# A routed expert layer in float32: 64-row units, and 129 to 192 rows of one expert in one body

## The reference

```python
logits = (hf @ router_w) + router_b
top_v, top_i = lax.top_k(logits, 4)             # 32 experts, 4 per token
gates = jax.nn.softmax(top_v, axis=-1)
...
gu = xb @ w_gu[e] + b_gu[e]                     # 1024 -> 2048
gate = jnp.minimum(gu[:, :1024], 7.0)
up = jnp.clip(gu[:, 1024:], -7.0, 7.0)
act = (up + 1.0) * (gate * jax.nn.sigmoid(1.702 * gate))
y = act @ w_down[e] + b_down[e]                 # 1024 -> 1024
out = jnp.zeros((n_tok, d)).at[buf_tok].add(y * buf_w[:, None])
```

## Time and profile before

| | |
|---|---|
| median of 3 runs | 2874.4 us (2848.94 to 2881.16) |
| the profiled execution | 2873.04 us |
| its span, first to last instruction | 2871.3 us |
| PE busy, share of the span | 2514.8 us, 88% |
| PE weight loads busy | 2049.8 us, 71% |
| DVE, ACT, POOL busy | 54%, 41%, 14% |
| mean granted TensorE clock | 0.898 of 2.4 GHz |
| DMA, mean over the span | 201 GB/s |
| stage 6, first matmul to last split | 1054 to 2791 us |

### The profile page before, as it was taken

The page is one execution under the profiler, slowest core; times in us unless marked ns, Lnnn a source line. Parts: engine busy times, 40 slices in busy tenths (PEclk is TensorE's granted clock), DMA queues, the critical chain, the costliest instruction groups (busy, mean ns, idle before and its releaser), DMA issues. The chain is left out here.

```text
span 2871.3 us, 35294 instructions
## 1 busy us (share of the span) xinstructions
PE 2514.8 (88%) x11411; PEld 2049.8 (71%) x11412; DVE 1557.2 (54%) x1705; ACT 1163.9 (41%) x1355; POOL 406.4 (14%) x423
## 2 busy tenths in 40 slices
PE   4899765899959529999999999999999999999980
PEld 4788654677748428888788888888877788878860
DVE  4411075433331425577855585575688755867545
ACT  4112142222221024456644474454566645655430
POOL 1420023110010150001100010000011100101004
PEclk8999888555579759999999999999999999999995
DMA  3132212700023166688976697686799966988658
GB/s 127 68 108 84 85 33 57 282 1 1 0 83 110 63 213 195 212 265 296 364 240 201 206 336 241 202 295 202 259 367 368 359 205 226 360 283 296 227 172 351
DMA packets 429684, 577.36 MB, mean 201 GB/s; under 512 B 28989, under 2 KB 308670, under 8 KB 429630
## 3 DMA queue, kind: packets, MB, share of 16 engines
q1 hardware_dynamic: 414494, 525.25, 55.0%
q0 software_dynamic: 15136, 51.40, 4.7%
HBM read 509.31 MB, written 67.29 MB: 201 GB/s over the span
## 5 line engine op out<-in xcount | busy, mean ns | idle before, releaser
L1386 DVE TENSOR_TENSOR VL<-RAW,VH 128x2048 fp32r<-128x2048 f32 x389 | 883.3, 2286 | 273.6 <-ACT VH L1381 272.7
L1381 ACT ACTIVATE VH<-RAW 128x2048 fp32r<-128x2048 f32 x390 | 728.7, 1912 | 148.2 <-DMA RAW<-in_expert_w_gate_up 92.6
L164 PE MATMUL banks<-VH,TL 128*128 128x512 f32 x1504 | 587.9, 391 | 0.0
L162 PE MATMUL banks<-VH,TH 128*128 128x512 f32 x1504 | 587.4, 391 | 0.0
L163 PE MATMUL banks<-VL,TH 128*128 128x512 f32 x1504 | 586.9, 390 | 0.0
L163 PEld LDWEIGHTS banks<-VL,TH 128*128 128x128 f32 x1504 | 282.8, 188 | 62.0
L164 PEld LDWEIGHTS banks<-VH,TL 128*128 128x128 f32 x1504 | 282.7, 188 | 60.7
L162 PEld LDWEIGHTS banks<-VH,TH 128*128 128x128 f32 x1504 | 283.5, 189 | 54.0
L162 PE MATMUL banks<-VH,AH 128*128 128x512 f32 x752 | 297.4, 395 | 11.7 <-DVE AL L1554 11.7
L164 PE MATMUL banks<-VH,AL 128*128 128x512 f32 x752 | 293.9, 391 | 0.0
L163 PE MATMUL banks<-VL,AH 128*128 128x512 f32 x752 | 293.3, 390 | 0.0
(11 more groups left out here) (276 smaller groups left out, 2874.9 us busy)
## 6 DMA issues: line engine op xcount, KB each, us to landing
RAW<-in_expert_w_gate_up SPq DMA_DIRECT2D x264, 1024.0 KB
RAW<-in_expert_w_down SPq DMA_DIRECT2D x130, 1024.0 KB
dY<-zeros SPq DMA_DIRECT2D x32, 512.0 KB, 10.9
dY<-yb SPq DMA_DIRECT2D x62, 256.0 KB
RAW<-in_w_in SPq DMA_DIRECT2D x6, 2048.0 KB, 8.7
dY<-yb SPq DMA_DIRECT2D x68, 128.0 KB
xin<-in_x SPq DMA_DIRECT2D x8, 512.0 KB
RAW<-in_w_out SPq DMA_DIRECT2D x2, 2048.0 KB
```

Of the source, the lines that this page charges most:

```text
L162: pe.matmul(o, lh, rh, start=start, stop=False)
L164: return pe.matmul(o, ll, rh, start=False, stop=stop)
L1381: act.activation(VH[:, i, ks], RAW[:, i, ks], ACT.Copy).then_inc(s_hi, 1)
L1386: dve.tensor_tensor(VL[:, i, ks], RAW[:, i, ks], VH[:, i, ks].bitcast(f32), ALU.subtract).then_inc(s_w, 1)
```

## The change

Rows are counted in units of 64 instead of blocks of 128. A table entry covers up to three units; an expert with more gets a second entry. An entry with one or two units runs narrow(), which is the one-block body as before. An entry with three units (129 to 192 rows) runs wide(), which takes the place of the two-block body. In wide() the gate and up columns are computed the other way round: 128 weight columns are stationary, and the tokens stream, rounded and rest beside each other (T2 holds both, 2 x 192), so that VH meets 384 columns and VL the 192 rounded ones. The two halves of the sum stand side by side in PSUM. ACT adds the bias to the right one (Identity with a bias per partition, from btT), DVE adds the left one to it (zz). The result has the experts' inner index on the partitions already, so that the transposes L1617 and the gate and up bias matmuls are gone. The down columns are as before, with 128 and then 64 stationary rows (A2). The next entry's tokens are turned in columns 4 and 5 of both bodies, the first 128 and then 64 rows.

The core of the diff:

```diff
+UN = 64
+NW = 3 * UN
+SBMAX = S * TOPK // UN + NE
+SLOTS = (SBMAX + 2) * UN
+SSB = S * TOPK // NW + NE
...
-                for j in range(1, S // P):
-                    link(dve.scalar_tensor_tensor(out=nb[:], in0=cnt, scalar=float(j * P), in1=nb[:], op0=ALU.is_gt, op1=ALU.add))
+                for j in range(1, S // UN):
+                    link(dve.scalar_tensor_tensor(out=nb[:], in0=cnt, scalar=float(j * UN), in1=nb[:], op0=ALU.is_gt, op1=ALU.add))
...
-                for j in range(2, S // P, 2):
+                for j in range(3, S // UN, 3):
...
-                sp.dma_start(tokr[0:SBMAX], dTok.rearrange("(s p) a -> s (p a)", p=P)).then_inc(s_tk, 16)
+                units = dTok.rearrange("(s p) a -> s (p a)", p=UN)
+                for i in range(2):
+                    sp.dma_start(tokr[0:SBMAX, i * UN:(i + 1) * UN], units[i:i + SBMAX]).then_inc(s_tk, 16)
...
+                    pool.tensor_copy(bcur[:], btT[:, :, :, bass.ds(e, 1)].rearrange("p g i a -> p g (i a)")).then_inc(s_bcur, 1)
...
             @block.scalar
+                def pair_hi(s, i):
+                    act.wait_ge(s_a, s * G2 + (2 + i + 1))
+                    act.activation(A2[:, 0, i], qa[:, i % 2, 0:NW], ACT.Copy, scale=1.0 / ALPHA).then_inc(s_ahi, 1)
...
+                def wide(s):
+                    begin(s)
+                    act.wait_ge(s_bcur, s + 1)
+                    for i in range(G2):
+                        b = i % 2
+                        act.wait_ge(s_mm, s * N2 + (i + 1))
+                        act.activation(lo2[:, b, 0], ps[2 * b][:, NW:2 * NW], ACT.Identity, bias=bcur[:, 0, i:i + 1])
+                        act.activation(lo2[:, b, 1], ps[2 * b + 1][:, NW:2 * NW], ACT.Identity, bias=bcur[:, 1, i:i + 1]).then_inc(s_ea, 1)
+                        if i >= 1:
+                            pair_hi(s, i - 1)
+                        act.wait_ge(s_up, s * G2 + (i + 1))
+                        act.activation(sg[:, b, 0:NW], zz[:, b, 0], ACT.Silu, scale=ALPHA).then_inc(s_sg, 1)
+                        if i == G2 - 1:
+                            pair_hi(s, i)
+                        if b == 1:
+                            round_next(s, i // 2)
+                    for c in range(GU, NCH):
+                        tokens_hi(c - GU, s * 2 + (c - GU + 3))
...
             @block.vector
+                def wide(s):
+                    for i in range(G2):
+                        b = i % 2
+                        dve.wait_ge(s_ea, s * N2 + (i + 5))
+                        dve.tensor_tensor(zz[:, b], bank_pairs[b].rearrange("p (g n) -> p g n", g=2)[:, :, 0:NW], lo2[:, b], ALU.add).then_inc(s_up, 1)
+                        dve.wait_ge(s_up, s * G2 + (i + 1))
+                        dve.tensor_scalar(u1[:, b, 0:NW], zz[:, b, 1], LIMIT + 1.0, 1.0 - LIMIT, ALU.min, ALU.max).then_inc(s_clip, 1)
+                        if i >= 1:
+                            pair_lo(s, i - 1)
+                        dve.wait_ge(s_clip, s * G2 + (i + 1))
+                        dve.wait_ge(s_sg, s * G2 + (i + 1))
+                        dve.scalar_tensor_tensor(out=qa[:, b, 0:NW], in0=sg[:, b, 0:NW], scalar=TOP, in1=u1[:, b, 0:NW], op0=ALU.min, op1=ALU.mult).then_inc(s_a, 1)
+                        if i == G2 - 1:
+                            pair_lo(s, i)
+                        if b == 0:
+                            second_half(s, i // 2)
+                        else:
+                            first_half(s, i // 2)
...
             @block.tensor
+                def begin(s):
+                    pe.wait_ge(s_x, s * 2 + 2)
+                    pe.wait_ge(s_hot, s + 1)
...
+                def narrow(s):
+                    begin(s)
+                    for c in range(NCH):
+                        if c >= GU:
+                            tokens(c - GU, s * 16 + 32, s * 2 + (c - GU + 2))
...
+                def wide(s):
+                    begin(s)
+                    for i in range(G2):
+                        c, j = i // 2, i % 2
+                        if i < 2:
+                            pe.wait_ge(s_ea, s * N2 + (2 * i + 2))
+                        else:
+                            pe.wait_ge(s_up, s * G2 + (i - 1))
+                        for k in range(KT):
+                            if j == 0 and k % HK == 0:
+                                pe.wait_ge(s_w, s * N2 + (2 * c + 1 + k // HK))
+                            for g in range(2):
+                                o = ps[2 * j + g]
+                                col = slice(g * HC + j * P, g * HC + (j + 1) * P)
+                                if k == KT - 1:
+                                    pe.matmul(o[:, 0:NW], VL[:, c % 3, k, col], T2[:, 0, k], start=False, stop=False)
+                                last = pe.matmul(o[:, 0:2 * NW].rearrange("p (a n) -> p a n", a=2), VH[:, c % 3, k, col], T2[:, :, k], start=k == 0, stop=k == KT - 1)
+                                if k < KT - 1:
+                                    pe.matmul(o[:, 0:NW], VL[:, c % 3, k, col], T2[:, 0, k], start=False, stop=False)
+                        last.then_inc(s_mm, 1)
+                    pe.sem_inc(s_aT, G2)
```

More of the change, by code:

```diff
@@ L1322, in _ @@
                 pe.matmul(ps[3][:, 0:SSB + 1], ones[:], diag[:], start=True, stop=True).then_inc(s_exp, 1)
-                pe.wait_ge(s_tk, 16)
+                pe.wait_ge(s_bt, 2)
+                for g in range(2):
+                    for i in range(2 * GU):
+                        c, j = i // 2, i % 2
+                        rows, at = slice(64 * (c // 3), 64 * (c // 3) + NE), (c % 3) * CH + g * HC + j * P
+                        q, n = c // 3, 6 - 4 * (c // 3)
+                        last = pe.transpose(ps[4 + q][:, (g * n + i % 6) * NE:(g * n + i % 6 + 1) * NE], braw[rows, at:at + P], ident[rows, rows])
+                last.then_inc(s_bT, 1)
+                pe.wait_ge(s_tk, 32)
                 pe.transpose(ps[2][:, 0:SBMAX], tokr[0:SBMAX], ident[0:SBMAX, 0:SBMAX]).then_inc(s_tT, 1)
@@ L1401, in stage6, with height, superblocks @@
         G2, N2 = 2 * GU, 2 * NCH
-        def items(c, nh):
-            return [(h, c * nh + h) for h in range(nh)]
-        def superblocks(eng, body):
+        def height(h):
+            return P if h == 0 else UN
+        def superblocks(eng, narrow, wide):
             n = eng.value_load(nblk[0:1, 0:1], min_val=1, max_val=SSB)
@@ L1412, in superblocks @@
                     with eng.If(two > 0):
-                        body(s, 2)
+                        wide(s)
                     with eng.Else():
-                        body(s, 1)
+                        narrow(s)
                 with eng.Else():
@@ L1451, in _ @@
                     load(sp, c + 3, e0)
-                n = superblocks(sp, body)
+                n = superblocks(sp, narrow, wide)
                 for i in range(3):
@@ L1542, in _ @@
+                tokens_hi(0, 1)
+                tokens_hi(1, 2)
                 act.activation(warm[:], onec[:], ACT.Silu).then_inc(s_warm, 1)
-                superblocks(act, body)
+                superblocks(act, narrow, wide)
             @block.vector
@@ L1591, in _ @@
                 tokens_lo(0, 1)
-                superblocks(dve, body)
+                tokens_lo(1, 2)
+                superblocks(dve, narrow, wide)
             @block.tensor
@@ L1620, in body, with bias_in, turned @@
[L1620 to L1626 removed]
+                def bias_in(o, c, m):
+                    return pe.matmul(o, hot_e[:, c // 3, 0:m], btab[:, (c % 3) * CH:(c % 3 + 1) * CH], start=True, stop=False)
+                def turned(s, c):
+                    pe.wait_ge(s_a, s * G2 + (2 + (c + 1) * 2))
+                    pe.wait_ge(s_act, s * G2 + (2 + max(0, c - 1) * 2))
+                    for j in range(2):
+                        last = pe.transpose(ps[4 + c % 2][:, j * P:(j + 1) * P], qa[:, c % 2, j * P:(j + 1) * P], ident[:])
+                    last.then_inc(s_aT, 2)
@@ L1659, in _ @@
                 tokens(0, 16)
-                superblocks(pe, body)
+                tokens(1, 16, 1)
+                superblocks(pe, narrow, wide)
     YR = 4
```

318 lines of the change are left out of this document (171 added, 147 removed).

## The result

The changed kernel takes 2750.0 us (median of 4 runs, 2739.7 to 2754.2); the kernel before, with its runs beside it, 2873.8 us (2848.9 to 2881.2). The ratio is 0.957, 95% interval 0.953 to 0.962: 4.3% faster. The forecast was 2736 us in a range of 2695 to 2785.

The account below looks back on a forecast made before the run. PE was taken to bound the two-block bodies, the weights' transfer by DMA the late one-block ones. From 2873.0 us, -169 (wide), +27.5 (narrow) and +4.3 (rest) gave 2736 us, range 2695 to 2785.

Parts of the forecast that it names:

- The wide body: Stage 6, PE-bound: 61.0 us against 72.3 for the two-block body, 11.3 less fifteen times, -169 us.
- the check of the sum against the old body: Two-block body on PE: matmuls 68.0, transposes 3.5 and some 0.8 for uncovered loads give the marked 72.3 us.
- The pair: Wide gate and up: 384-column stream 0.173 plus load-bound 192-column one 0.112, 0.285 us; 128 pairs take 36.5 us.
- rival A: Wide body's weight loads wholly hidden: pairs of 0.266, 2.4 us less per body, 2700 us; chance 0.13.
- Rival B: Wide body's loads don't overlap, each matmul waits 0.188 us: body 11.6 us longer than forecast, 2911 us; chance 0.06.
- ACT and DVE: Wide body's chain: 9.5 to 9.9 us a column against PE's 9.1, 3.2 us of slack, so nothing counted.
- Rival D: ACT and DVE chain bounds the wide body: at 10.5 us a column 2.3 us more a body, 2771 us; chance 0.09.
- The narrow bodies: One-block bodies lengthen: +2.7 us in seven PE-bound ones, 8.6 us over ten later ones, together +27.5 us.
- The wait: Narrow body, column 5: PE's transposes wait 1.9 us for column 4's TL, part of the +2.7 us.
- Rival C: Waits add up: the 2.7 us come on top in ten DMA-bound one-block bodies, 18 us more, 2754 us; chance 0.13.
- The rest: Outside the bodies: routing 1.8 us, second table read 0.5, empty turns 2, together +4.3 us.
- The five empty turns: End of stage 6: loop runs 53 times instead of 48, 0 to 3 us, taken as 2.

Follow-up runs that it names:

- kernel 5: The changed kernel plus eight unused 512-column bias matmuls ahead of column 5's wait in the narrow body: 2737.2 us, ratio 0.952.
- kernel 3: The changed kernel with the VL matmul cut from 192 to 64 columns: 2804.5 us in two runs.
- kernel 6: The changed kernel with DVE making zz twice for each group of a wide body: 2763.4 us in one run.
- kernel 2: The kernel before, with only a PE wait for column 4's TL added ahead of column 5 in one-block bodies: 2903.3 us, ratio 1.009.
- kernel 9: The changed kernel with 33 instead of 53 turns of the loop over the table: 2731.4 us, ratio 0.948.
- kernel 8: The kernel before, with the wait for TL ahead of column 5 in one-block bodies and eight unused 64-row transposes behind it: 2914.7 us, ratio 1.020.
- kernel 4: The changed kernel with the VL matmul widened from 192 to 256 columns, the extra being other data: 2768.7 us in two runs.
- kernel 1: The changed kernel with the narrow body's eight 64-row transposes moved behind the first half of column 5's product: 2724.9 us, ratio 0.948.
- kernel 7: kernel 1 with the narrow body's 64-row token splits set ahead of column 5's weights on ACT and DVE: 2721.0 us, ratio 0.951.

## Why the prediction came out as it did

**The wide body: right.** 61.05 us against 61.0. In kernel 5, whose clock does not fall, the fifteen wide intervals are 169.1 us shorter than before, where -169 was forecast. That is partly luck: the first two intervals gained 8.6 and 9.7 instead of 11.3, and four wide ones that had taken 73.7 before gained 12.5. Nor did the check of the sum against the old body test every term: its 0.8 for uncovered loads is what was missing to 72.3, and no row is named for it. The pair is what was claimed, 0.285 us, though the matmul records don't show its halves. PE and PEld inside a wide body of the changed kernel:

```profile
1499.89 0.36 PE L1763 MATMUL banks<-T,VH 128*128 128x384 f32 x1
1499.92 0.19 PEld L1765 LDWEIGHTS banks<-T,VL 128*128 128x128 f32 x1
1500.09 0.25 PE L1765 MATMUL banks<-T,VL 128*128 128x192 f32 x1
1500.10 0.19 PEld L1763 LDWEIGHTS banks<-T,VH 128*128 128x128 f32 x1
1500.18 0.36 PE L1763 MATMUL banks<-T,VH 128*128 128x384 f32 x1
1500.20 0.19 PEld L1765 LDWEIGHTS banks<-T,VL 128*128 128x128 f32 x1
```

Matmul starts are 0.20 behind a 384 and 0.09 behind a 192, not 0.17 and 0.11 as the prediction said they would be; the loads start 0.18 behind a VL's and 0.10 behind a VH's, near the two terms. In kernel 3 matmul starts are 0.26 and 0.04 apart while those of the loads stay: under load-bound matmuls it was the records of the loads that kept the rhythm. Read by matmul starts alone, the row would have spoken for rival A (0.093 and nothing waited for), which kernel 3 excludes: with 64 columns the body stays at 61.37, and by A's rule it would be 128 × 0.053 us (128 columns at 2.4 GHz) = 6.8 shorter.

The Trainium skill ("TensorE: Matmul & The Clock Gate", LDWEIGHTS) gives P / 1.2 ns for a load of P columns, by which 128 columns are an estimated 107 ns; the 0.11 us of kernel 3 agrees. The Trainium skill ("Perfetto Trace Analysis", Identifying the Most-Contended Engine) would judge headroom by the sum of the load times over the window. Here 372 loads of 0.19 us sum to 71 us in a window of 61.00, so that sum can't be the measure. A recorded load overlaps the next by 0.08 in kernel 3, and with overlaps counted once the loads are busy for 53.83 us. Rival B (2911 us) had counted on the old body's mean of 59.28 us for 332 loads, but the overlap grew.

**ACT and DVE: right to count nothing, but not because slack covered a drift.** The groups by form of the changed kernel (busy us, mean ns | idle before) that answer to the estimates from the earlier trace rows:

```profile
L1657 DVE TENSOR_TENSOR zz<-banks,lo 128x384 f32<-128x384 f32 x120 | 66.9, 558 | 52.9 <-ACT lo L1586 47.3
...
L1585 ACT ACTIVATE lo<-banks,bcur 128x192 f32<-128x192 f32 x120 | 49.6, 413 | 154.7 <-PE banks L1763 154.7
```

zz takes 0.558 (0.55 estimated), ACT's read of PSUM 0.413 (0.33, too low). ACT waits for PE 154.7 us in total here, so the chain is early, not late: the drift of 0.4 to 0.8 a column that the prediction feared is absent, each column takes 9.11 us, and kernel 6 added 4.5 us to the chain for 0.5. So the chain of 9.5 to 9.9 us a column was estimated too long, though ACT's read in it was too short; which of its links in truth overlap I did not take apart. Rival D is out.

**The narrow bodies: the step that failed is what follows the wait.** The wait (1.84 us against 1.9) and the sum of +2.7 are right: 38.77 from 35.95 is +2.8. The late ones stayed at 38.7 rather than 39.2; without falls the seventeen sum to +23.7 us (kernel 5) where +27.5 was forecast. The forecast has a slip there too: from 37.6 to 39.2 is +1.6 and not +1.4, which for four bodies is 0.8 us more. Rival C, waits that add up on the DMA-bound bodies, is out: in the changed kernel such a body without a fall takes 38.7 as before, and kernel 2's +1.0 is its second wait, for the one-hot, which the changed kernel doesn't have. What the prediction lacked is a price for PE's standstill beyond its own length. It named the wait, and what is queued behind it, at full clock. The falls cost 16.5 us by kernel 5's span, or 11 × 1.55 = 17 by the intervals, nine tenths of the miss of 18.

**The rest: mis-sized in one term.** Stage 5 answers to the earlier trace rows; DVE's chained instructions and the read of the slot table, now:

```profile
988.83 3.36 DVE L1250 SCALAR_TENSOR_TENSOR nb<-tsum,nb 128x32 f32<-128x32 f32 x15
...
1046.49 0.81 SPq L1202 DMA_DIRECT2D tokr<-dTok  x2
```

Fifteen for seven, 3.36 us for 1.54, and from the first counting matmul to the first token transpose it is 73.7 us instead of 71.6: +2.2, where 1.8 and 0.5 were forecast. Another 1.9 us came about ahead of stage 5, in code that the change does not touch. The five empty turns were taken as 2 us in a range of 0 to 3; the tail grew by 4.7, and at kernel 9's 0.68 a turn they are 3.4 of it. The 10.6 us over 16 turns, 0.66 each, had been the measure all along; I took less because I thought something else lay in them.

With the price of the falls and the turns at 0.68 the sum would have been 2736 + 16.5 + 1.4 = 2754 us, against 2754.2 for the profiled execution. That near an agreement has errors in it that cancel: -4 in the narrow bodies against +1.9 ahead of stage 5 and the rest of the tail.

## What to carry to other kernels

Where a PE stream gets a wait, price two things: its own length, and the clock behind it. Look whether transposes stand right behind it, and put them where their data has long been there; or, if they can't be moved, fill the wait. A stationary operand under a stream shorter than its own load (here 0.11 us for 128 columns, a stream of somewhere between 192 and 256) costs the load: a pair of a short and a long stream was still worth it, since 128 pairs of 0.285 us took the place of 192 matmuls of 0.227, 36.5 us for 43.5. If you add a wait to one engine, look also at what it pushes the others' work against: in kernel 2 POOL's one-hot went from 0.94 to 4.88 us beside DVE's splits, and PE waited again. And count a loop's unused turns: they are cheap one by one, but lie bare at the end.

## What the runs showed of the hardware that was not expected

The granted clock falls to half for 3.4 us after 1.84 us of idle PE and eight 64-column transposes: at ten of 17 places in the changed kernel, and as often in kernel 8; at eleven, ten, twelve and nine of 17 in kernels 3, 4, 6 and 9, which have the same wait and transposes. It does not after 1.75 us of idle time with products right behind (none of 17, kernel 2), nor after the transposes with PE busy ahead of them (none of 17 in kernels 5, 1 and 7). Longer idle times with products right behind stand at the start of the second body. A fall came behind 2.39 us (kernel 1), 2.37 (kernel 9), 2.18 (changed kernel) and 2.13 (kernel 7), and one of 6.8 us with the 3.02 of kernel 6; none came behind 2.14 (kernel 4), 2.10 (kernel 3) and 1.64 (kernel 5). Since 2.13 brought one and 2.14 did not, something besides the idle time decides. What that is, and which of the 17 places are hit, is open; kernel 9 has the same bodies as the changed kernel and other places.

With 64-column streams in place of 192 the clock rose from half to full 68 us later (kernel 3, 1137.7 us against 1069.9), while PE was busy throughout from 1066 us on. That is one trace. What decides when it rises is open too.

A short matmul has a floor, and little below it is free: from 192 to 256 columns it cost 0.009 us more each, and from 192 to 64 the body became 0.3 us longer, not shorter, which I can't explain.

The same one-hot on POOL took 0.94 us in each of the 17 narrow bodies of the kernel before and 4.88 in each of kernel 2, where it ran beside three of DVE's splits and ended 0.7 us behind the last of them.
